# Three products of a weight tile side by side in the hybrid and attention mixers of a decoder trunk

## What is computed

```python
for i in range(DEPTH):                                   # DEPTH = 2
    h = h + 0.5 * swiglu(rms_norm(h, norm_ff1[i]), ffn1_gate[i], ffn1_up[i], ffn1_down[i])
    hn = rms_norm(h, norm_mix[i])
    if i % 2 == 0:
        z, xbc, dt_raw, gate_b, x_b = jnp.split(hn @ hyb_w_in[j], HYB_SPLITS, axis=-1)
        ...                                              # y_a = ssd_mixer(...), y_b = rglru_mixer(...)
        h = h + jnp.concatenate([y_a, y_b], axis=-1) @ hyb_w_out[j]
    else:
        h = h + diff_attention(hn, dif_w_qkv[j], ..., dif_w_o[j], lambda_init, cos, sin)
    h = h + 0.5 * swiglu(rms_norm(h, norm_ff2[i]), ffn2_gate[i], ffn2_up[i], ffn2_down[i])
return rms_norm(h, final_norm)
```

## Time and profile before

| | |
|---|---|
| time, median of 3 runs | 1065.91 us (1065.07 to 1067.28) |
| time of the profiled execution | 1065.55 us |
| its span | 1063.7 us |
| mean granted TensorE clock | 0.995 |
| busy: PE, weight loads (PEld), DVE, ACT, POOL | 1050.4, 944.8, 792.3, 611.4, 51.1 us |
| the mixers: hybrid, attention | start at 195.55 and 752.58 us of the span |

### The profile page before, as it was taken

One profiled execution on the slowest core, in us unless ns is written; L12 is line 12 of the kernel. 1 busy time (PEld: TensorE's weight loads), 2 busy tenths in 40 slices (PEclk: granted clock), 3 DMA queues, 4 the chain that ended last, 5 costly groups with the idle time before them and its releaser, 6 DMA issues.

```text
span 1063.7 us, 18486 instructions
## 1 busy us (share of the span) xinstructions
PE 1050.4 (99%) x6678; PEld 944.8 (89%) x6678; DVE 792.3 (74%) x1137; ACT 611.4 (57%) x980; POOL 51.1 (5%) x70
## 2 busy tenths in 40 slices
PE   9999999999999999999999999999999999999997
PEld 8888888899998998888888888888999998888886
DVE  6788776679868878887666888776699578888653
ACT  6555554468976665555445665543456756656541
POOL 0200011100000000000111000011100000000011
PEclk9999999999998999999999999999999999999999
DMA  8866775549644656667755666685566446667671
GB/s 250 213 195 193 211 205 162 156 124 259 175 114 125 200 156 191 189 194 206 208 158 159 196 196 189 197 218 165 146 169 165 120 127 200 190 195 204 188 200 40
DMA packets 369283, 190.14 MB, mean 179 GB/s; under 512 B 5920, under 2 KB 368704, under 8 KB 369232
## 3 DMA queue, kind: packets, MB, share of 16 engines
q1 hardware_dynamic: 368976, 188.89, 63.0%
q0 software_dynamic: 256, 0.59, 0.3%
HBM read 187.86 MB, written 1.07 MB: 178 GB/s over the span
## 4 chain that ended last, share of the span: by engine, by line
PE 94%; ACT 3%; DVE 2%; issue 1%; DVEq 0%; ACTq 0%
PE psum L217 45%; PE psum L220 24%; PE psum L201 7%; PE psum L205 7%; PE psum L202 6%; PE psum L1898 1%; ACT whi L185 1%; PE psum L1523 1%; DVE wlo L190 1%; PE psum L966 0%; DVE arena L1195 0%; PE psum L956 0%; PE psum L883 0%; PE psum L939 0%; PE psum L957 0%
## 5 line engine op out<-in xcount | busy, mean ns | idle before, releaser
L190 DVE TENSOR_TENSOR wlo<-raw,whi 128x1024 fp32r<-128x1024 f32 (+1 forms) x324 | 416.9, 1305 | 76.1 <-ACT whi L185 74.7
L185 ACT ACTIVATE whi<-raw 128x1024 fp32r<-128x1024 f32 (+1 forms) x324 | 354.0, 1113 | 35.0 <-PE psum L205 26.3
L217 PE MATMUL psum<-xn,whi 128*128 128x512 f32 x1408 | 354.3, 393 | 0.5 <-DVE xn L307 0.5
L217 PEld LDWEIGHTS psum<-xn,whi 128*128 128x128 f32 x1408 | 253.4, 189 | 46.7 <-issue 0.6
L220 PEld LDWEIGHTS psum<-xn,wlo 128*128 128x128 f32 x1408 | 192.4, 190 | 13.8
L220 PE MATMUL psum<-xn,wlo 128*128 128x256 f32 x1408 | 196.9, 282 | 0.0
L217 PE MATMUL psum<-hid,whi 128*128 128x512 f32 x704 | 171.8, 391 | 0.0
L217 PEld LDWEIGHTS psum<-hid,whi 128*128 128x128 f32 x704 | 128.1, 189 | 24.0
L201 PE MATMUL psum<-xn,whi 128*128 128x256 f32 x480 | 122.1, 292 | 0.9 <-ACT whi L185 0.9
L202 PE MATMUL psum<-xn,whi 128*128 128x256 f32 x480 | 118.9, 285 | 0.0
L510 ACT ACTIVATE arena<-arena 128x256 f32<-128x256 f32 x88 | 36.8, 419 | 112.4 <-DVE arena L574 112.4
(11 more groups left out here) (230 smaller groups left out, 873.1 us busy)
## 6 DMA issues: line engine op xcount, KB each, us to landing
raw<-in_ffn_gate SPq DMA_DIRECT2D x88, 512.0 KB, 3.9
raw<-in_ffn_up SPq DMA_DIRECT2D x88, 512.0 KB, 3.9
raw<-in_ffn_down SPq DMA_DIRECT2D x64, 704.0 KB, 4.6
raw<-in_hyb_w_in SPq DMA_DIRECT2D x36, 512.0 KB, 4.9
raw<-in_dif_w_qkv SPq DMA_DIRECT2D x24, 512.0 KB, 4.5
raw<-in_hyb_w_out SPq DMA_DIRECT2D x16, 512.0 KB, 4.7
raw<-in_dif_w_o SPq DMA_DIRECT2D x8, 512.0 KB, 4.1
hid<-cs_rows SPq DMA_DIRECT2D x4, 512.0 KB, 6.9
```

The costliest lines, as they stand in the source:

```text
L185: act.activation(whi[:, s, 0:k * P], raw[:, s, 0:k * P], ACT.Copy).then_inc(s_whi, 1)
L190: dve.tensor_tensor(wlo[:, s, 0:k * P], raw[:, s, 0:k * P], whi[:, s, 0:k * P].bitcast(F32), ALU.subtract).then_inc(s_wlo, 1)
L217: pe.matmul(acc, hi[:, j, :], x[:, t, :, :], start=start and j == 0, stop=False)
```

## The change

In `multiply`, the wait for the block's remainder moves to its start, behind the wait for its rounded part. One loop then runs over the tiles, with three products for each: hi weight with hi activations, hi weight with lo activations, lo weight with hi activations. Before, a first loop ran the two hi-weight products for all tiles of the block (or part), and a second one the lo-weight products. The number of instructions, their shapes and the accumulated terms stay; `multiply_wide` is not touched.

```diff
             hi, lo = tile_of(whi, s, k), tile_of(wlo, s, k)
             pe.wait_ge(s_whi, b + 1)
+            pe.wait_ge(s_wlo, b + 1)
             for j in part or range(k):
                 t = k0 + j
                 if need:
                     need(t)
                 pe.matmul(acc, hi[:, j, :], x[:, t, 0, :], start=start and j == 0, stop=False)
                 pe.matmul(acc, hi[:, j, :], x[:, t, 1, :], start=False, stop=False)
-            pe.wait_ge(s_wlo, b + 1)
-            for j in part or range(k):
-                mm = pe.matmul(acc, lo[:, j, :], x[:, k0 + j, 0, :], start=False, stop=stop and j == k - 1)
+                mm = pe.matmul(acc, lo[:, j, :], x[:, t, 0, :], start=False, stop=stop and j == k - 1)
             if j == k - 1:
                 mm.then_inc(s_blk, 1)
```

## The result

The changed kernel takes 1069.81 us in the median of 8 runs (1069.27 to 1070.74), the kernel before 1066.30 us in 8 runs on the same chip (1065.07 to 1068.12). The ratio is 1.0032, 95% interval [1.0021, 1.0043]: 3.4 us slower, 2.2 to 4.6. The profiled execution took 1069.27 us at a span of 1067.5.

A forecast was written before the change was run, and what follows sets the result against it. TensorE, busy nearly throughout, bounds the kernel, so its waits are paid unless later swallowed. 1.18 + 1.68 + 0.24 + 0.10 - 0.87 + 1.18 = +3.5 us gives 1069.4 us; range 1065.8 to 1071.6, likeliest case 1068.5 to 1070.4.

The forecast's parts named there:

- The order itself at 0: All moved products: same number, each loading its own weights, seams free at 120 ns, so the new order costs 0.
- Blocks 1, 6, 8, 10: Hybrid blocks with late remainders: 1.18 us at 1, 1.68 at 6, no wait at 8, 0.24 at 10.
- the 1.68 us of block 6: Hybrid block 6: split ends at 219.29 against a start at 217.66, 1.63 + 0.05 us.
- the 0.24 us of block 10: Hybrid block 10: TensorE, already 2.86 us behind, ends 3.10 behind, so only 0.24 us more.
- the wait of near 1.2 us at block 10: Sign in the new profile: TensorE waits near 1.2 us for L190 ahead of hybrid block 10.
- Blocks 30 and 32: Hybrid: late by 0.14 and 1.12 us, but swallowed by TensorE's waits for ScalarE; 0.1 us left.
- Block 36: Hybrid block whose tiles wait for L1333: three products follow the last tile instead of eight remainder products; -0.87 us.
- Attention: Block 1 costs 1.18 us; every other remainder is ready before its block starts, output blocks 0.
- the first two rivals: Clock's fall at the group sums goes away, 1066.0 us (22%); further fall ahead of block 6, 1071.1 or 1072.8 (12%).
- the first rival: Group sums: work filling the idle time keeps the clock up, saving up to 3.4 us, 1066.0, no change; 22%.
- The pace rival: Mixed products run faster than 120 ns, 5 ns each over 2016 products, 10 us won, 1059 us; 7%.
- the swallowed waits: 0.5 us less lost in each mixer's block 1, blocks 6 and 10 gain too; 1067.3 us, no change; 9%.

The follow-up runs named there:

- block 32 alone: Kernel before with the new code in hybrid block 32 only; ratio 0.9998 [0.9987, 1.0009] to before.
- TensorE kept busy ahead of block 6: Changed kernel plus thirteen further 256-column products, result dropped, ahead of hybrid block 6; 1070.04 us, ratio 1.0025 to before.
- the wait alone: Kernel before with only the early wait for the remainder, its two loops kept; 1070.22 us, ratio 1.0031 [1.0020, 1.0043] to before.
- block 6 alone: Kernel before with the new code in hybrid block 6 only; ratio 1.0001 [0.9989, 1.0013] to before.
- the moved sums with the old block 36: Kernel before with group sums moved into the middle of block 34, old code in every block; 1063.06 us, ratio 0.9969 to before.

## Why the prediction was right

**The bound.** Right. Pace stayed at 120 ns, and apart from 0.7 us in the first stretch the span changed by TensorE's waits, block 36's work behind its last tile, and the clock. Not every wait went to the end: those of blocks 30 and 32 were swallowed, as forecast.

**The order itself at 0.** Right: within 0.6 ns for each product by the times of the kernels with the new order in 76 blocks and in one, and within 0.1 ns by their profiles.

**Blocks 1, 6, 8, 10.** Right in sum: +3.25 us against +3.10, with 42.35 to 42.40 us from block 0 to 11 in the five kernels that keep the early wait in blocks 1 and 10, whatever they do at block 6. The term was built as a chain, and that the prices of its links belong to the chain and not to the blocks is what the experiments add: giving back the 1.68 us of block 6 saves nothing, and the 0.24 us of block 10 is 1.97 when it stands alone. One sign did not come: the wait of near 1.2 us at block 10 is not in the changed kernel's profile, where the slow clock had made TensorE late. With the clock at full it is there, 1.22 and 1.29 us, and the sum is the same either way.

**Blocks 30 and 32.** Right: -0.01 against +0.10, and block 32 alone costs nothing.

**Block 36.** Right, mis-sized by 0.1: 0.76 us where 0.87 were forecast. The first four tiles were done before the fifth was there, but the product behind the wait for the fifth was a long one, its successor starting 0.22 us later (339.60) and not 0.12, which the forecast of 0.36 us for each tile left out:

```profile
339.38 0.39 PE L202 MATMUL psum<-hid,whi 128*128 128x256 f32 x1 [0.19 <-DVE hid L1332]
```

**Attention.** Block 1 was right: 4.05 us to the next block against 2.88. The step that failed is "In the rest of attention every remainder is ready before its block starts" (with the sentence before it that has attention's output blocks "find their tiles and remainders ready"). It put at 0 a term that measured 0.9 us. Of the 84 blocks not seven but eight were late. The rows of before that I should have put side by side are these:

```profile
856.94 0.76 DVE L432 SCALAR_TENSOR_TENSOR h<-psum,h 128x256 f32<-128x256 f32 x2 [2.83 <-PE psum L205]
857.62 2.35 DVE L190 TENSOR_TENSOR wlo<-raw,whi 128x1024 fp32r<-128x1024 f32 x2
...
858.18 0.28 PE L201 MATMUL psum<-hid,whi 128*128 128x256 f32 x1
```

The first of the two splits ends near 858.8, block 28 starts at 858.18. As in block 6, VectorE had other work ahead of the split that waits for TensorE's preceding block (the residual, L432), so the price is paid whatever went before: 0.64 us idle, and 0.87 with what the modelled end hides. With the old code in this block alone the 0.9 us were gone.

**The total.** The number is closer than the reasoning earned. The terms with block 28 make 4.4 us, and 3.4 [2.2, 4.6] was measured; that a forecast without block 28, 3.5 us, met it so nearly is luck. In the two profiled executions the stretches that the prediction is about make +3.25 - 0.01 - 0.76 + 0.01 + 2.1 = +4.6 us, the shorter fall of the clock takes off 1.6 and the later start adds 0.7. The repeated executions point the same way. Two kernels that cost the same by the stretches, the one with TensorE kept busy ahead of block 6 and the one with the old code at block 6, had a mean granted clock of 0.9955 over 12 executions each, against 0.9937 and 0.9938 of before beside them, and their mean span is 2.95 us longer. At the 0.7 to 1 us for each 0.001 that the executions of before show, that is an estimate of 4.2 to 4.7 us at like clock. Why the clock stands higher in them is not shown. The likeliest case's own range was also wider than its allowances make: sums of 3.0 to 4.0 us give 1068.9 to 1069.9, not 1068.5 to 1070.4.

**The rivals.** The clock's falls did shift, as the first two rivals had it, and together: in the profile of the changed kernel half of the fall at the group sums went, and one came at block 6. The reason of the first rival, that filling the idle time ahead of the sums keeps the clock up, did not hold: with the new code in block 32 alone that idle time is filled, and the windows of 0.97 and 0.69 still make 6.8 us of fall. In the changed kernel the fall at block 6 costs nearly nothing, since block 10 would have waited; the prediction had priced it at up to 1.7 us. That a longer wait at block 6 brings it about is likely but not settled: it is in the profiles of the changed kernel, of the wait alone and of block 6 alone, not in those that have no such wait (13 products in it, or the old code at 6), and also not in the one with the old code at attention's block 28, which has the wait. The pace rival fell, and so did the swallowed waits: block 1 cost 1.17 to 1.18 us in both mixers.

## What to carry to other kernels

Moving a wait forward costs nothing where the awaited work is done, so list for every place the end of that work against the new start, to the last block of every phase: the one missed row here was worth 0.9 us. The late places don't add up. Follow them as one chain with two clocks, one for the engine that waits and one for the engine that is waited for, and ask at each place whether the late engine was itself waiting for the first. A wait that disappears later (here ahead of the group sums) is where a delay is given back.

## What the runs showed that I had not expected

The clock of TensorE goes with most of the spread of this kernel. Of the kernel before, on one chip, an execution with a mean granted clock of 0.996 had a span of 1062.9 us, those with 0.992 spans near 1066.9: about 1 us for each 0.001, over the same code. A fall of 3.4 us shows as 1.1 to 1.6 us in the stretch that it falls in (1.6 behind the group sums, 1.1 in the old block 36: 5.25 us against 4.14), unless a wait that would have followed takes it in. TensorE fell to 1.2 GHz in or right behind the one-column products in every profile but that of the moved sums with the old block 36, where it fell at block 36's waits instead; a further fall stood at the old block 36 in three profiles (the wait alone, block 6 alone, block 32 alone). The Trainium skill's page "TensorE: Matmul & The Clock Gate", Part 1, says that activity releases the throttle. The window with thirteen products in the wait stayed at 1.00, which agrees with it but does not test it, since one profile with the same wait left empty (the old code at attention's block 28) has 1.00 there too.
